# Hybrid mixer and sparse experts on one core: the output projection in three f16 products, and router logits taken from x and the mixer output

## The chip, the cores and the metric

The program runs on one core of a Trainium2 chip. The metric is the device time of one execution in microseconds; each figure is the median of several executions. The engines are TensorE (PE; PEld is its weight load), VectorE (DVE), ScalarE (ACT), GpSimd (POOL) and SyncE (SP), each with an instruction queue of its own, run in order; they meet through semaphores.

## What is computed

The reference, cut to what matters here (one sequence of 4096 tokens behind 16 learned ones, D = 1024):

```python
def hybrid_mixer(u, w_in, ..., lru_out_norm, ..., dn_out_norm, w_out):
    proj = u @ w_in                      # 3080 columns: xb gb q k v z b_logit a_logit
    y_lru = rmsnorm(rglru_group(xb, gb, ...), lru_out_norm)        # 512 wide
    y_dn = gated_deltanet_group(q, k, v, z, ..., dn_out_norm)      # 512 wide, per-head norm, times silu(z)
    return jnp.concatenate([y_lru, y_dn], axis=-1) @ w_out

h = h + hybrid_mixer(rmsnorm(h, mix_norm), ...)
h = h + hierarchical_moe(rmsnorm(h, ffn_norm), router_group_w, router_group_b,
                         router_expert_w, router_expert_b, w_gate, w_up, w_down)
out = rmsnorm(h, final_norm)[:, 16:]
```

The router takes a softmax over 4 groups, the best group, and its best two of 8 experts: 36 logits a token, from rmsnorm(h, ffn_norm) times 36 columns, plus a bias.

## The kernel before, in words

The work has four stages: a set-up, a mixer loop over 33 tiles of 128 tokens, a loop over 83 blocks of up to 128 tokens by expert, and a last loop that gathers, adds and norms the rows. The change touches the first two.

**Set-up** (L290 to L408, and the first steps of the loop). SP issues the loads of x, of w_in in six column groups, of w_out and last of the router's columns w_rt (L303). All engines then meet at a barrier (`retire`, L408). In step i = -1 the weights of w_in are split into two f16 halves in place: for each of the six groups, DVE's `scale_of` (L962) searches the largest weight, with a transpose and a one-row product on PE (`largest`, L488) to bring it across partitions; ACT's `high_halves` (L758) writes eight high halves into spare rooms; DVE's `low_halves` (L986) subtracts them; POOL copies the high halves back (L1254). Every product with w_in is then three f16 products: low weight with high x, high with high, high with low x.

**Mixer loop** (L97: steps i = -2 to 34, the middle ones in a hardware loop). One step works on five tiles at different points (class `Step`): F norms, transposes and splits x of tile i + 3; P projects tile i + 2; G runs the recurrences of tile i + 1; O multiplies the mixer output of tile i - 1 by w_out; R routes tile i - 2. All parts are active in steps 3 to 30. The order on each engine is written by hand. PE's body (L594 on) lays the six column projections (`project`, L495; L514 is its product) between the six levels of the delta rule's triangular solve: `level_y` (L569, product L580) and `level_x` (L583, product L591). In a level PE's product goes to DVE (a masked copy and a transpose, L1022 and L1028) or to ACT (a copy, L789), which return the operand of the next, while PE projects a quarter of a column group (24 products). The parts that the change touches:

- `w_out_part` (L550): 8 blocks of the mixer output times 2 halves of w_out, 16 f32 products of 512 columns (L564, two rows of the trace each) into the two banks bO. It is the last part of PE's body; the product for the norm of the recurrent branch (L752) stands behind its first eighth.
- DVE adds the bank to the residual ht (L1081), ACT norms it (L828), DVE scales it (L1110). PE transposes it in 8 products (L656, after level 2), DVE scales it by ffn_g to hT (L1146), and PE multiplies it by w_rt: 8 f32 products on 36 columns, 16 rows (L671, after level 4). DVE adds the bias (L1159) and picks groups and experts (L1165 to L1214). In the last steps, without P and G, this chain stands by itself.
- `z` is projected last, into the bank pj[1] (L531), then the 8 columns of beta and a (L546), then PE transposes x (L745). ACT's queue has, in this order: the two copies of the transposed x to f16 (L907), silu of z (L912, semaphore z_done), the square of q.
- The delta rule's output yt is transposed by PE after level 5 (L694) and copied by ACT (L876). DVE forms yl, the other half of the projection's operand, after level 3 (L1153); POOL's yg (L1290) overwrites its input and so waits for it; POOL's la (L1293) comes after yg, and ACT's square (L866), gate (L871) and tanh (L880) follow from them.

## Time and profile before

| | us |
|---|---|
| median of 3 runs | 3845.93 |
| lowest, highest | 3840.99, 3847.76 |
| profiled execution | 3841.46 |
| its span, first to last instruction | 3839.8 |
| PE busy, share of the span | 3449.2, 90% |
| DVE, ACT, POOL busy | 2168.8 (56%), 1462.9 (38%), 773.4 (20%) |
| mean granted TensorE clock | 0.961 |

The page cuts the span in 40 slices of 96 us. PE is busy 90% or more from the fourth slice to the twenty-seventh (the mixer loop) and again from the thirtieth on (the experts, where DMA is busy too); the last two slices are DMA. A timeline row merges neighbouring instructions of one line and gives the start, the length from the first start to the last end, and the count; in brackets stands the idle time before it and what ended it. Rows of PE overlap a little, so that a cost is best read from start to start.

### The profile page before, as it was taken

What the parts mean: (1) busy time and instruction counts of PE and PEld (TensorE: products, weight loads), DVE (VectorE), ACT (ScalarE), POOL (GpSimd) and SP (SyncE); (2) the same over time, 40 slices, a digit from 0 to 9 for tenths busy, and PEclk for the clock granted to TensorE, in tenths of its full rate; (3) what the DMA queues carried; (4) which work ended last, traced back from release to release, by engine and by line L of the source; (5) the groups of instructions that cost most, each with busy time, mean ns of one, the idle gap of its engine ahead of it and who ended that gap; (6) DMA issues with size and microseconds to landing.
All of it is one profiled execution on the core that took longest, in us unless ns stands there. A gap on an engine that the chain in (4) does not pass through costs nothing. (4 is left out here: it accounts for less than half of the span.)

```text
span 3839.8 us, 79823 instructions
## 1 busy us (share of the span) xinstructions
PE 3449.2 (90%) x28912; PEld 2563.9 (67%) x28913; DVE 2168.8 (56%) x6010; ACT 1462.9 (38%) x3048; POOL 773.4 (20%) x843
## 2 busy tenths in 40 slices
PE   0688999999999999999999999985899999999910
PEld 0687888888788878878887887873454454544400
DVE  4755776676677667667766776763322222222267
ACT  3444444544454444445444444532011111111168
POOL 2311221211122121212112221210111111111055
PEclk9999999999999999999999999997999999999955
DMA  5000100010010001001000100022465545456289
GB/s 197 7 7 18 49 30 33 33 44 27 33 44 33 30 30 49 27 33 44 33 27 33 49 27 33 32 90 115 153 237 204 193 153 196 153 191 224 110 337 379
DMA packets 94235, 358.72 MB, mean 93 GB/s; under 512 B 15953, under 2 KB 16210, under 8 KB 81874
## 3 DMA queue, kind: packets, MB, share of 16 engines
q1 hardware_dynamic: 49330, 219.35, 15.2%
q0 software_dynamic: 26032, 77.69, 5.7%
q10 hardware_dynamic: 18800, 60.70, 3.9%
q8 instruction: 46, 0.75, 0.1%
q14 instruction: 27, 0.22, 0.0%
HBM read 246.52 MB, written 111.18 MB: 93 GB/s over the span
## 5 line engine op out<-in xcount | busy, mean ns | idle before, releaser
L514 PE MATMUL pj<-uT,W 128*128 128x128 f16 x15840 | 979.8, 220 | 0.0
L514 PEld LDWEIGHTS pj<-uT,W 128*128 128x128 f16 x15840 | 937.4, 98 | 44.1 <-issue 38.4
L1483 PE MATMUL bA<-W,uT 128*128 x1328 | 588.6, 596 | 6.7 <-issue 4.0
L1483 PEld LDWEIGHTS bA<-W,uT 128*128 128x128 f32 x1328 | 248.2, 192 | 288.2 <-issue 288.2
L1570 DVE TENSOR_TENSOR W<-W,bA 128x256 f32<-128x256 f32 x83 | 34.9, 421 | 563.0 <-ACT W L1517 563.0
L1470 PE MATMUL pj<-W 128*128 x664 | 298.8, 593 | 1.8 <-ACT W L1522 1.8
L564 PE MATMUL bO<-W,yl 128*128 128x512 f32 x512 | 237.8, 598 | 0.0
L564 PE MATMUL bO<-W,yt 128*128 128x512 f32 x512 | 230.2, 592 | 0.0
L789 ACT ACTIVATE qh<-bA 128x256 f32<-128x256 f32 x198 | 76.6, 387 | 400.1 <-PE bA L580 400.1
L580 PE MATMUL bA<-dec,Mt 128*128 128x128 f32 x1584 | 220.4, 282 | 5.1 <-DVE dec L1028 3.3
L591 PE MATMUL bB<-X,qh 128*128 128x128 f32 x1584 | 221.0, 283 | 2.9 <-ACT qh L789 2.9
L1517 ACT ACTIVATE W<-bA 128x256 f32<-128x256 f32 x83 | 32.0, 385 | 463.5 <-PE bA L1483 463.5
L1470 PEld LDWEIGHTS pj<-W 128*128 128x128 f32 x664 | 120.1, 191 | 121.5 <-issue 121.5
L580 PEld LDWEIGHTS bA<-dec,Mt 128*128 128x128 f32 x1584 | 193.5, 193 | 8.3 <-DVE dec L1028 4.7
L591 PEld LDWEIGHTS bB<-X,qh 128*128 128x128 f32 x1584 | 193.2, 192 | 4.2 <-ACT qh L789 4.2
L1308 POOL DMA_INDIRECT idx_tab<-toki,posi x64 | 63.8, 997 | 650.5 <-DVE posi L1223 581.1
L531 PE MATMUL pj<-W,uT 128*128 128x512 f16 x792 | 191.5, 379 | 0.0
L564 PEld LDWEIGHTS bO<-W,yt 128*128 128x128 f32 x512 | 97.3, 190 | 122.4 <-issue 122.4
L1505 ACT ACTIVATE W<-pj 128x512 f32<-128x512 f32 x83 | 49.6, 597 | 329.5 <-PE pj L1470 329.5
L1022 DVE COPY_PREDICATED X<-lvl,bB 128x256 f32<-128x256 uint8 x165 | 81.6, 495 | 161.0 <-PE bB L591 159.6
L564 PEld LDWEIGHTS bO<-W,yl 128*128 128x128 f32 x512 | 93.3, 192 | 93.7 <-issue 93.7
L1545 DVE COPY W<-pj 128x512 f32<-128x512 f32 x83 | 57.4, 691 | 156.1 <-PE pj L1470 156.1
(346 smaller groups left out, 5892.1 us busy)
## 6 DMA issues: line engine op xcount, KB each, us to landing
y_rows<-W ACTq DMA_DIRECT2D x83, 512.0 KB
W<-w_gate SPq DMA_DIRECT2D x32, 1024.0 KB
W<-w_up SPq DMA_DIRECT2D x32, 1024.0 KB
W<-w_down SPq DMA_DIRECT2D x32, 1024.0 KB
x_in<-xm SPq DMA_DIRECT2D x33, 512.0 KB
ht<-xm SPq DMA_DIRECT2D x32, 512.0 KB, 3.5
h_rows<-ht SPq DMA_DIRECT2D x32, 512.0 KB, 2.6
u_rows<-ht SPq DMA_DIRECT2D x32, 512.0 KB, 2.7
```

The lines of the kernel that those rows point to most:

```text
L514: mm = pe.matmul(pj[g % 2][:, j, :], w16[:, k, w_half(w_high, COL[GROUPS[g]], 512, j * P, P)], (ul if low_u else uh)[:, k, :], start=(k == ...
L531: mm = pe.matmul(flat(pj[1]), u[:, k, :], w16[:, k, w_half(w_high, c, 512)], start=(k == 0 and n_pass == 0), stop=(k == KT - 1 and n_pass ...
L564: mm = pe.matmul(bOf[:, 512 * half:512 * half + 512], lhs, wo[:, j, 512 * half:512 * half + 512], start=(j == 0), stop=(j == 7))
L580: mm = pe.matmul(bA[:, h, :], Mt[:, h, :], T[:, h, :], start=True, stop=True)
L591: mm = pe.matmul(bB[:, h, :], Y[:, h, :], X[:, h, :], start=True, stop=True)
L789: nc.scalar.activation(first_half(Y, l), first_half(bA, l), ACT.Copy).then_inc(sem("Y_new"), 1)
L1022: a = nc.vector.copy_predicated(second_half(X, l), mask_of(l), second_half(bB, l))
L1308: pool.indirect_dma_start(out=idx_tab, out_offset=bass.IndirectOffsetOnAxis(ap=posi[:, a:a + 1], axis=0), in_=toki[:], in_offset=None).the ...
L1470: mm = pe.matmul(flat(pj[half]), hm2[:, j, :], w[:, j, 512 * half:512 * half + 512], start=(j == 0), stop=(j == 1))
L1483: mm = pe.matmul(bA[:].rearrange("p a b -> p (a b)").rearrange("p (g f) -> p g f", g=2), xT[:, k, :], w[:, k], start=(k == 0), stop=(k == ...
L1505: nc.scalar.activation(yo[par][:, 0:512], flat(pj[0]), ACT.Copy).then_inc(sem("yo_a"), 1)
L1545: nc.vector.tensor_copy(yo[par][:, 512:D], flat(pj[1])).then_inc(sem("yo_b"), 1)
```

## The change

Four things change together. w_out, times the norm gains, is split once into f16 halves in place (in step 1, half block by half block: ACT, DVE, POOL), and the mixer output is split in every tile, so that the projection is three f16 products into bO, unscaled by DVE as it adds the residual. The router's columns, times ffn_g, are folded: once through w_out (`router_through`: 8 blocks transposed by PE, copied by ACT, multiplied by PE), giving 36 more columns of the output projection, which go to pj[1]; and 36 columns on x, computed beside beta and a (44 columns in place of 8). The logits are the sum of the two, times the norm's factor. The transposes of the residual and its product with w_rt go. Beside these, buffers are renamed or shared (rnk becomes kh, hT becomes lath) and semaphores joined. The diff, cut to its core:

```diff
 # SP
                 sp.wait_ge(sem("bd_in"), 64)
+                sp.dma_start(gw, w_router.rearrange("(p k) n -> p k n", k=KT)).then_inc(sem("w_rt_in"), 16)
                 for g in GROUPS:
...
                 sp.dma_start(wo, w_out.rearrange("(k p) n -> p k n", p=P)).then_inc(sem("w_out_in"), 16)
-                sp.dma_start(w_rt[:], w_router.rearrange("(p k) n -> p k n", k=KT)).then_inc(sem("w_out_in"), 16)
...
                     if s.O:
-                        need(sp, sem("h_turned"), s.nR)
-                        settle(sp)
                         need(sp, sem("u_stored"), 32 * s.nR)
 # PE
+                def router_through(j):
+                    if j == 0:
+                        pe.wait_ge(sem("w_out_in"), 16)
+                        pe.wait_ge(sem("set_step"), GW_SET)
+                    need(pe, sem("wo_copied"), j)
+                    for k in range(KT):
+                        mm = pe.transpose((bA, bB)[k // 4][:, k % 4, :], wo[:, j, k:D:KT], ident[:])
+                    mm.then_inc(sem("wo_turned"), 1)
+                    pe.wait_ge(sem("wo_copied"), j + 1)
+                    c = 512 + (NG + NE) * j
+                    for k in range(KT):
+                        mm = pe.matmul(bOf[:, c:c + NG + NE], turned_room(j, k // 4)[:, k % 4, :], gw[:, k, :],
+                                       start=(k == 0), stop=(k == KT - 1))
+                    mm.then_inc(sem("wo_through"), 1)
...
                             need(pe, sem(free), v)
+                            if g == 1:
+                                need(pe, sem("lg_raw"), s.nR)
...
                     for k in range(KT):
-                        for n_pass, (w_high, u) in enumerate(((False, uh), (True, uh), (True, ul))):
-                            mm = pe.matmul(bB[:, 0, 0:2 * H], u[:, k, :], w16[:, k, w_half(w_high, c, 2 * H)],
+                        for n_pass, (part, u) in enumerate(((1, uh), (0, uh), (0, ul))):
+                            mm = pe.matmul(bB[:, 0, 0:2 * H + NG + NE], u[:, k, :], wba[:, k, part, :],
...
+                            need(pe, sem("h_ready"), s.nR)
+                            need(pe, sem("z_done"), s.nP)
-                        for j in (2 * m, 2 * m + 1):
-                            lhs = yl[:, j, :] if j < 4 else ydT[:, j - 4, :]
-                            mm = pe.matmul(bOf[:, 512 * half:512 * half + 512], lhs, wo[:, j, 512 * half:512 * half + 512],
-                                           start=(j == 0), stop=(j == 7))
+                        for part, whole in ((0, (False, True)), (1, (True,))):
+                            y = yl16[:, part, j, :] if j < 4 else yd16[:, part, j - 4, :]
+                            for half in range(2):
+                                for w_high in whole:
+                                    pe.matmul(bOf[:, 512 * half:512 * half + 512], y, wo16[:, j, w_half(w_high, 512 * half, 512)],
+                                              start=(j == 0 and not w_high), stop=(j == 7 and part == 1))
+                            for w_high in whole:
+                                mm = pe.matmul(pj[1][:, 0, 0:NG + NE], y, wog[:, j, 0 if w_high else 1, :],
+                                               start=(j == 0 and not w_high), stop=(j == 7 and part == 1))
...
                     if isinstance(s.i, int) and s.i == -1:
+                        largest(0, bT)
                         for g in range(len(GROUPS)):
-                            largest(g)
+                            largest(1 + g, bT)
+                            if 0 < g < 5:
+                                router_through(2 * g - 2)
+                                router_through(2 * g - 1)
+                    if isinstance(s.i, int) and s.i == 1:
+                        largest(1 + len(GROUPS), bO)
+                        largest(2 + len(GROUPS), bO)
...
                     project(s, 1, 3)
-                    if s.R:
-                        need(pe, sem("u2_ready"), s.nR)
-                        for k in range(KT):
-                            mm = pe.transpose(bO[:, k, :], ht[:, k:D:KT], ident[:])
-                        mm.then_inc(sem("h_turned"), 1)
                     level_y(s, 3)
                     project(s, 2, 0)
                     level_x(s, 3)
+                    if s.O:
+                        need(pe, sem("yt_ready"), s.nO)
+                        need(pe, sem("kd_ready"), s.nG)
+                        for h in range(H):
+                            mm = pe.transpose(bT[:, h, :], yt[:, h, :], ident[:])
+                        mm.then_inc(sem("yd_full"), 1)
...
                     level_x(s, 4)
-                    if s.R:
...
-                        for k in range(KT):
-                            mm = pe.matmul(bTf[:, 0:NG + NE], hT[:, k, :], w_rt[:, k, :], start=(k == 0), stop=(k == KT - 1))
 # ACT
+                def turned(j):
+                    act.wait_ge(sem("wo_turned"), j + 1)
+                    need(act, sem("wo_through"), j - 1)
+                    for n, bank in enumerate((bA, bB)):
+                        a = nc.scalar.activation(turned_room(j, n), bank[:], ACT.Copy)
+                    a.then_inc(sem("wo_copied"), 1)
+                def o_high(n):
...
+                    need(act, sem("o_split"), n - 3)
+                    nc.scalar.activation(o_room(n), wo[:, k, 512 * half:512 * half + 512], ACT.Copy,
+                                         scale=gso[:, k:k + 1]).then_inc(sem("o_high"), 1)
...
                             high_halves(g)
+                            if 0 < g < 5:
+                                turned(2 * g - 2)
+                                turned(2 * g - 1)
...
                     level_y(s, 3)
+                    if s.O:
+                        need(act, sem("yd_full"), s.nO)
+                        nc.scalar.activation(yd16[:, 0], bT[:], ACT.Copy).then_inc(sem("yd_high"), 1)
                     level_y(s, 4)
+                    if s.O:
+                        need(act, sem("yl_raw"), s.nO)
+                        nc.scalar.activation(yl16[:, 0], yg[:], ACT.Copy).then_inc(sem("yl_high"), 1)
...
-                        nc.scalar.activation(ydT[:], bT[:], ACT.Copy).then_inc(sem("ydT_ready"), 1)
...
+                    if isinstance(s.i, int) and s.i == 1:
+                        for n in range(16):
+                            o_high(n)
 # DVE
+                def out_scale():
+                    dve.wait_ge(sem("wo_through"), KT)
+                    step(nc.vector.tensor_reduce(wmx[:], wo, AX, ALU.max, apply_absolute_value=True))
...
+                    halves_of(wog[:], gw)
...
+                        router_columns()
                         scale_of(0)
...
+                        y_gains()
...
-                            a = nc.vector.tensor_tensor(ht[:, c], ht[:, c], bOf[:, c], ALU.add)
+                            a = nc.vector.scalar_tensor_tensor(out=ht[:, c], in0=bOf[:, c], scalar=odsc[:, 0:1], in1=ht[:, c],
+                                                               op0=ALU.mult, op1=ALU.add)
                         a.then_inc(sem("h_ready"), 1)
+                        need(dve, sem("lg_ready"), s.pR)
+                        nc.vector.scalar_tensor_tensor(out=lg[:], in0=pj[1][:, 0, 0:NG + NE], scalar=gdsc[:, 0:1], in1=lgx[:, 0, :],
+                                                       op0=ALU.mult, op1=ALU.add).then_inc(sem("lg_raw"), 1)
...
                     level_x(s, 3)
-                            a = nc.vector.tensor_tensor(hT[:, k:k + 4, :], bO[:, k:k + 4, :], rows(fg[:, k:k + 4]), ALU.mult)
                     conv(s, 1, qs, 0, 1)
-                            a = nc.vector.scalar_tensor_tensor(out=yl[:, j, :], in0=yg[:, j, :], scalar=lcol[:, 4, j:j + 1],
-                                                               in1=lrs[:], op0=ALU.mult, op1=ALU.mult)
+                        nc.vector.tensor_tensor(yg[:], yg[:], cols(lrs[:]), ALU.mult).then_inc(sem("yl_raw"), 1)
                     level_x(s, 4)
+                        nc.vector.tensor_tensor(yd16[:, 1], bT[:], yd16[:, 0], ALU.subtract).then_inc(sem("yd_ready"), 1)
                     conv(s, 1, qs, 2, 3)
+                        nc.vector.tensor_tensor(yl16[:, 1], yg[:], yl16[:, 0], ALU.subtract).then_inc(sem("yl_ready"), 1)
                     level_x(s, 5)
...
+                    if isinstance(s.i, int) and s.i == 0:
+                        out_scale()
+                    if isinstance(s.i, int) and s.i == 1:
+                        for n in range(16):
+                            dve.wait_ge(sem("o_high"), n + 1)
...
+                                                           in1=o_room(n), op0=ALU.mult, op1=ALU.subtract).then_inc(sem("o_low"), 1)
 # POOL
+                    if isinstance(s.i, int) and s.i == 1:
+                        for n in range(16):
+                            pool.wait_ge(sem("o_low"), n + 1)
+                            nc.gpsimd.tensor_copy(wo16[:, k, w_half(True, 512 * half, 512)], o_room(n)).then_inc(sem("o_split"), 1)
```

`router_columns`, `y_gains` and `out_scale` are chains of small DVE instructions, each waited for, on [128 x 8] or [128 x 288] operands, with one or two `largest` trips to PE; `out_scale` also reads all of w_out (8192 elements a partition).

## Rows read from the trace of the kernel before

**Rows 1.** Windows of the mixer stage: busy us (x instructions) by engine, granted clock.
```profile
core 0: us, PE busy (x) PEld busy (x) DVE busy (x) ACT busy (x) POOL busy (x), PEclk, DMA share, GB/s
1000.00:2000.00 1000.00, 1000.00 (x10639) 842.95 (x10637) 705.84 (x2169) 464.99 (x1021) 197.31 (x187) 1.00 0.09 35
```

**Rows 2.** Timeline of PE over one tile: start us, length us, line, tiles, xcount.
```profile
1000.95 1.11 PE L656 MATMUL bO<-ident,ht 128*128 128x128 f32 x8
1001.90 1.06 PE L580 MATMUL bA<-dec,Mt 128*128 128x128 f32 x8
...
1011.00 1.87 PE L671 MATMUL bT<-w_rt,hT 128*128 128x36 f32 x16
1012.70 1.14 PE L677 MATMUL bC<-xc,wr_bd 128*128 128x128 f32 x8
...
1038.77 1.46 PE L531 MATMUL pj<-W,uT 128*128 128x512 f16 x6
1040.07 0.75 PE L546 MATMUL bB<-W,uT 128*128 128x8 f16 x24
1040.67 0.69 PE L745 MATMUL bC<-ident,x_in 128*128 128x128 f32 x4
...
1041.63 1.88 PE L564 MATMUL bO<-W,yl 128*128 128x512 f32 x4
...
1048.73 3.60 PE L564 MATMUL bO<-W,yl 128*128 128x512 f32 x8
1052.16 3.60 PE L564 MATMUL bO<-W,yt 128*128 128x512 f32 x8
```

**Rows 3.** Timeline of PE in an early tile that has no residual yet.
```profile
188.06 1.50 PE L514 MATMUL pj<-uT,W 128*128 128x128 f16 x24
189.89 1.16 PE L580 MATMUL bA<-dec,Mt 128*128 128x128 f32 x8 [0.33 <-DVE dec L1028]
```

**Rows 4.** Timeline of ACT behind the transposes of x, tile of rows 2.
```profile
1041.83 0.60 ACT L907 ACTIVATE uT<-bC 128x512 f16<-128x512 f32 x1 [6.12 <-PE bT L745]
...
1042.80 0.69 ACT L912 ACTIVATE zs<-pj,dsc 128x512 f32<-128x512 f32 x1
```

**Rows 5.** Timelines of DVE and of PE at level 2 of the tile above.
```profile
1070.50 0.68 DVE L1122 TENSOR_TENSOR ot<-bA,eg 128x512 f32<-128x512 f32 x1
...
1071.33 1.13 PE L580 MATMUL bA<-dec,Mt 128*128 128x128 f32 x8
```

**Rows 6.** Timeline of DVE in the set-up and at the start of step 1.
```profile
51.75 4.41 DVE L973 TENSOR_REDUCE wmx<-W 128x8 f32<-128x4096 f32 x1
...
58.14 0.16 DVE L980 TENSOR_SCALAR dsc<-bT 128x1 f32<-128x1 f32 x1 [0.67 <-PE bT L493]
...
240.36 0.16 DVE L1042 SCALAR_TENSOR_TENSOR g<-al,ga 128x4 f32<-128x4 f32 x1 [6.08 <-ACT ga L805]
```

**Rows 7.** Timelines of ACT in the set-up and of PE in the last steps.
```profile
63.29 0.71 ACT L764 ACTIVATE vt<-W,gs 128x512 f16<-128x512 f32 x1
...
2622.23 1.97 PE L656 MATMUL bO<-ident,ht 128*128 128x128 f32 x8 [6.11 <-DVE ht L1110]
2625.58 3.63 PE L671 MATMUL bT<-w_rt,hT 128*128 128x36 f32 x16 [1.38 <-DVE hT L1146]
```

**Rows 8.** Timeline of SP: the last DMA that it issues before the loop.
```profile
36.47 3.67 SPq L303 DMA_DIRECT2D w_rt<-w_router  x1
```

**Rows 9.** Timeline of PE behind two idle times, and a window (columns: rows 1).
```profile
137.79 2.08 PE L677 MATMUL bC<-xc,wr_bd 128*128 128x128 f32 x8 [3.95 <-DVE xc L951]
...
162.36 1.12 PE L605 MATMUL bA<-rnq,ones 128*128 128x512 f32 x2 [1.41 <-ACT rnq L915]
...
135.00:146.00 11.00, 8.21 (x80) 8.14 (x81) 10.72 (x36) 1.80 (x7) 2.85 (x4) 0.69 0.01 2
```

**Rows 10.** Timeline of POOL beside DVE's eight subtractions, and behind them.
```profile
122.15 5.85 POOL L1254 COPY W<-rnq 128x512 f16<-128x512 f16 x1 [8.12 <-DVE W L991]
127.95 0.61 POOL L1254 COPY W<-rnk 128x512 f16<-128x512 f16 x1
```

More of the change, by code:

```diff
@@ L189, in hymba_block @@
         fg = sb("fg", [P, KT])
-        dng = sb("dng", [P, P])
+        dnc = sb("dnc", [P, 1])
+        gain = sb("gain", [P, KT])
+        gso = sb("gso", [P, KT])
+        sd = sb("sd", [P, 1])
+        rdsc = sb("rdsc", [P, 2])
+        odsc = sb("odsc", [P, 2])
+        gdsc = sb("gdsc", [P, 2])
         nexp_a = sb("nexp_a", [P, H])
@@ L916, in body @@
                         need(act, sem("conv"), 16 * s.nP)
[L917 removed]
+                        nc.scalar.activation(vs[:], vs[:], ACT.Silu).then_inc(sem("qkv_silu"), 1)
                     nc.scalar.preload_act_table_set("natural_log_exp_and_others")
```

283 lines of the change are left out of this document (170 added, 113 removed).

## The prediction, made before the result was known

> **What bounds the kernel now.** I read the windows by stage first, then the timeline of TensorE (PE) over one token tile, then ACT and DVE beside it. Between 1000 and 2000 us PE is busy 1000 of 1000 us at a granted clock of 1.00, DVE 706 and ACT 465 [rows 1]. So in the mixer stage, which covers some 33 token tiles and about 2600 us, every microsecond that leaves PE's stream leaves the time, as long as nothing new makes PE wait. The expert stage and the last stage run the same code after the change and are costed at nothing. The edit touches three places: the tile loop (32 times), the set-up before it, and the last two steps.
>
> **The tile loop, what is removed.** The output projection is 16 f32 products of 512 columns, each shown as two rows. Eight rows start 3.43 us apart [rows 2], so 32 rows are 13.7 us a tile. It becomes 48 f16 products of 512 columns. Six such products (z's, L531) take 1040.07 - 1038.77 = 1.30 us, 0.216 each, weight loads included [rows 2]: 48 are 10.4 us. The 24 router products on 36 columns are bounded by the 24 on 8 columns (1040.67 - 1040.07 = 0.60 us, 25 ns each) and by the 128-column f16 product: 24 of them fill a row of 1.50 [rows 3], and a row's length counts some 0.16 that the next start overlaps (L531's is 1.46 long, 1.30 to the next start), so 56 ns each. That is 0.6 to 1.3 us. I take 0.6, because 36 columns are nearer to 8 than to 128. Projection: 13.7 - 11.0 = **2.7 us saved**. The eight transposes of the residual (L656) go: 0.95 us (1000.95 to 1001.90). The router's 16 rows (L671) go: 1.70 us (1011.00 to 1012.70) [rows 2]. The beta columns grow from 8 to 44: 0 to 0.7 us by the same two bounds, I take 0. The mixer's transposes only move from after level 5 to after level 3. Gross: **5.4 us a tile**.
>
> **The tile loop, what it adds.** (1) The new logits go to pj[1], the bank that holds z. So the output projection now waits for z_done, and z_done is the activation that ACT issues after its two copies of the turned x. PE starts the projection at 1041.63 [rows 2], right behind the transposes of x; ACT starts the copies at 1041.83 and ends z at 1042.80 + 0.69 = 1043.49 [rows 4]. ACT's order cannot change, as its queue has the copies first. PE therefore stands still about **1.9 us** in each tile that projects, with everything behind it. What follows is a projection shorter by 2.7 us, so the next tile's start comes only 0.8 us earlier and ACT's chain (v's silu, the norms) still ends in time. (2) The transposes at L656 stood between one quarter of a projection and level 3. Three early tiles have no residual yet and show the gap without them: PE starts 24 products at 188.06 and the level only at 189.89, idle 0.33 for DVE's transpose [rows 3]; with the overlap of 0.16 that is lost too, **0.5 us** of the 0.95 comes back as a wait. (3) DVE runs without a pause into level 2: its product with eg ends at 1071.18 and PE's level starts at 1071.33 [rows 5]. The new DVE instruction that scales the logits stands ahead of it, and a small one that reads PSUM takes 0.16 [rows 6]: **0.2 us**. (4) The rest I cost at nothing. DVE loses two 512-column passes and four short ones, and gains two for the low halves and one for the norm; ACT swaps one copy for two. Both work under PE's products. The price if that cover goes is in the rivals. POOL's product yg, with la behind it on its queue, now waits for the low half at about level 5 instead of level 4; ACT's square, gate and tanh wait for it, and level 6 behind them. Laying the old durations end to end, ACT comes to level 6 just before PE needs it, by some tenths. SP loses one wait and issues the same DMAs.
>
> Per full step 5.4 - 1.9 - 0.5 - 0.2 = **2.8 us saved**. Full steps (all parts active) are i = 3 to 30: 28 x 2.8 = 79 us.
>
> **The edges of the loop.** Step 2: 2.7 - 1.9 = 0.8. Step 31, without x to turn, has almost no z wait: about 4. Steps 32 and 33 save the projection only: 5.5. In the last two steps PE waits, and the chain residual, transposes, hT, router lies open: the transposes start at 2622.23 and the router rows end at 2625.58 + 3.63 [rows 7]. That is 7 us gone from the last step, and 5 from the one before, which gets the new low halves in exchange. Sum 22 us saved.
>
> **The set-up, what it adds.** (a) DVE folds the router first: a dozen small instructions of 0.16 to 0.2, two trips to PE of 0.5 to 0.7 [rows 6], and passes over 288 columns of at most 0.5 each: +4.5 us in a stretch where DVE is the only bound. (b) w_rt was the last DMA that SP issued, and its issue took 3.67 [rows 8], while all engines wait for SP: now it is the first, so -3 (bounds 0 and -3.7). (c) Between the searches for the largest weight, PE turns two blocks of w_out and multiplies them, with ACT's copies between, four times. Such a gap is some 12.5 us of DVE work (a reduction of 4.41, eight subtractions of 0.7, a dozen small ones). ACT is free about 7 us into it, after its eight halves (the last at 63.29 [rows 7]). Then follow a copy pair (1.1), 16 router rows at the low clock (3.63), eight transposes (1.9) [rows 7], copies, 16 rows: 11 us, or 9 if the clock rises in between. So DVE waits about 4.5 us each time (bounds 0 and 6): +18. (d) Four more small instructions and some waits: +1. (e) At the end of step 0 DVE searches w_out: as much as two reductions of 4.41 [rows 6], some 18 small ones and four trips to PE, 16 us in all. DVE was idle 6.08 us there [rows 6], which leaves 10; and the next step's first two products, 512 columns each and some 1.1 us long [rows 9], now stand behind it at the low clock: +13 (bounds 8 and 16). (f) At the end of step 1, 16 half blocks go from ACT to DVE to POOL through four rooms. But POOL's copy of a half block, 0.61 alone, took 5.85 us while DVE ran eight such subtractions, 0.73 each [rows 10]. If the engines overlapped, DVE would set the pace, 16 x 0.73 = 12 us; one after the other they take 21. The row says the second, and ACT's 0.6 hides beside them: less the two or three us in which the next step's start waits for ACT's table load anyway, +16 (bounds 11 and 20). Rule of the Trainium skill, page "SBUF — State Buffer", section "Who interferes with whom": DVE with two SBUF inputs and GpSimd lock each other out for a whole instruction. By that rule this term is at its upper half, not at 11, and the row agrees with it.
> Set-up: 4.5 - 3 + 18 + 1 + 13 + 16 = **+49.5 us**.
>
> **Sum:** 49.5 - 79 - 22 = -52 us, rounded. The profiled execution took 3841.46 (span 3839.8), so it would take 3789; it stands 4.5 under the median of the three runs shown, 3845.93, and against that median I forecast **3793**.
>
> **The rivals.**
> *The clock falls at the new wait (slower).* After PE had idled 1.41 us its next two rows of 512 columns took 1.12 in all, about what they take at a granted clock of 1.00 (0.43 from start to start, and the end of the last); after 3.95 us, eight products took 2.08 instead of 1.14 [rows 2, 9], and the mean granted clock of that stretch of 11 us was 0.69, a mix of 1.2 and 2.4 GHz: up to 3.4 us of work lost. The new wait of 1.9 lies between the two idle times, nearer the harmless one. If it does cost 3 us each, 29 waits are +87: 3880. From 1.8 us a wait it eats the whole gain. Behind it: the Trainium skill, "TensorE: Matmul & The Clock Gate", Part 1, says that the clock is throttled unless activity holds it open; no row shows it doing so at 1.9 us. Chance 0.10.
> *More cover gone.* If the late yg, or DVE before levels 5 and 6, lacks its slack, PE waits another 1 us a tile, and the set-up terms come out near their upper ends: +28 and +14, 3835. For it: DVE is already the last to arrive at level 2 [rows 5]. Against: no level from 4 to 7 lets PE wait now [rows 1]. Chance 0.16.
> *The z wait costs nothing*, because what follows waits anyway: 28 x 1.9 = 53 less, 3740. Against it: PE never waits between 1000 and 2000 us [rows 1]. Chance 0.06.
> *The products are not cheaper*: if f16 weight loads showed between products, 0.1 us each, 48 would cost 15 us, not 10.4, and nothing is gained on PE: about 3920. L531's products, which load weights each time too, speak against it [rows 2]. Chance 0.02.
>
> **How the numbers follow.** The forecast has 0.66. Its own unknowns (set-up 20 to 64, gain a step 1.6 to 3.3) rarely all fall on one side: 3768 to 3820. Stretching to the cases beside it, with some 0.1 left out above and 0.08 below, gives 3760 to 3838. A measurement of this kernel can tell about 0.2%, 7.7 us. Faster: 0.66 + 0.06 + 0.12 of the third case = 0.84; same 0.05; slower 0.11.
>
> **What would show it.** PE's rows: 48 f16 rows of L564's kind at 0.216; a wait of 1.9 on ACT's z once a tile, the largest new wait; 0.5 on DVE at level 3; steps about 72.1 us apart. Before 400 us: DVE waits of 4 to 5 us on PE four times, and the first output projection about 50 us later than before. The granted clock stays near 1.00 between 400 and 2500 us. Wrong it would be if steps are over 74 us apart, if the clock falls, or if the set-up costs over 64 us.

## The result, and the profile after

The kernel after takes 3881.44 us (median of 4 runs, 3880.08 to 3885.57), the kernel before 3846.28 in the same comparison: a ratio of 1.0096, 95% interval 1.0078 to 1.0113. The change makes it slower by about 35 us, or 1%, where 53 us less were forecast.

Lines of its page, and of the page of before the one for the instruction queue, which nothing ahead of the prediction looked at:

```profile
span 3879.5 us, 81931 instructions
PE 3350.6 (86%) x29625; PEld 2503.3 (65%) x29626; DVE 2220.5 (57%) x6133; ACT 1512.9 (39%) x3145; POOL 805.3 (21%) x859
PEclk9988999999999999999999999997899999999955
q8 instruction: 282, 4.62, 0.5%
```

```profile
q8 instruction: 46, 0.75, 0.1%
```

PE is busy 99 us less than before (3350.6 against 3449.2): the work that was to go did go. But the span grew by 39.7. So the question is not what the new products cost but what PE now waits for. The window of [rows 1] gives the size of it:

```profile
1000.00:2000.00 1000.00, 937.61 (x10730) 792.23 (x10728) 707.50 (x2196) 476.16 (x1039) 199.53 (x184) 1.00 0.11 37
```

PE was never idle there before; now it is idle 62.4 us in 13.3 steps, 4.7 a step. The granted clock is 1.00 as before (the upper level, 2.4 GHz), so nearly all of the loss is idle time and not a slower clock. The waits of PE say where it is (what waited and its line, what ended the wait, us in total, times, longest). In them ot is DVE's product with eg, ahead of level 2, and dec is its transpose inside a level:

```profile
PE bO L604 <- ACT zs L976: 53.7, 30, 1.8
PE bA L623 <- DVE ot L1259: 41.8, 30, 1.8
...
PE bB L652 <- issue: 28.2, 26, 1.4
...
PE bA L623 <- DVE dec L1152: 16.1, 36, 1.7
```

Four waits, each once a step. The first was forecast at 1.9 us and is 1.84; the last at 0.33 and is 0.35. The second was forecast at 0.2 and is 1.38. The third wasn't forecast. Timeline of PE around the output projection, in a step of the loop; it answers to [rows 2]:

```profile
1015.51 0.76 PE L583 MATMUL bB<-wba,uT 128*128 128x44 f16 x24
...
1016.64 0.61 PE L781 MATMUL bT<-ident,x_in 128*128 128x128 f32 x4
1019.10 1.02 PE L604 MATMUL bO<-W,yl 128*128 128x512 f16 x4 [1.84 <-ACT zs L976]
1019.96 0.21 PE L607 MATMUL pj<-wog,yl 128*128 128x36 f16 x2
...
1030.34 0.18 PE L607 MATMUL pj<-wog,yt 128*128 128x36 f16 x1
1031.61 1.10 PE L652 MATMUL bB<-kh,ones 128*128 128x512 f32 x2 [1.09 <-issue]
```

```profile
1055.59 1.02 PE L602 MATMUL bB<-rnk,ones 128*128 128x512 f32 x2
```

The last row is of before. Read them from start to start. From the second four transposes of x to the first product of the next step are 1031.61 - 1016.64 = 14.97 us; before, the same stretch took 1055.59 - 1041.20 = 14.4. It should have been shorter by 2.6 (f16 in place of f32) and longer by 1.9 (z). It is some 1.3 us longer again, of which 1.09 is idle time ahead of L652, which is the first instruction of the hardware loop's body, and "issue" means that no semaphore of another engine explains it.

And DVE with POOL ahead of level 2, which answers to [rows 5] (L1244 is u2, the scaling of the residual; L1246 multiplies the logits by the norm's factor and adds the bias):

```profile
1045.21 0.73 DVE L1244 TENSOR_SCALAR ht<-ht,hst 128x1024 f32<-128x1024 f32 x1
1045.86 1.27 DVE L1246 SCALAR_TENSOR_TENSOR lg<-lg,hst,rb 128x36 f32<-128x36 f32 x1
...
1048.08 0.68 DVE L1259 TENSOR_TENSOR ot<-bA,eg 128x512 f32<-128x512 f32 x1
```

```profile
1045.32 1.75 POOL L1424 TENSOR_TENSOR gx<-gx,hh 128x512 f32<-128x512 f32 x1 [4.42 <-ACT hh L898]
```

The new operation on 36 columns takes 1.27 us, longer than u2 on 1024. It ends at 1047.13, where POOL's product ends (1045.32 + 1.75 = 1047.07).

The stores of h on SP's queue date the steps (the MOVE is in the loop's 27 steps alone):

```profile
L483 SPq DMA_DIRECT2D h_rows<-ht x32: 333/356/365, 442.7 to 2698.7; - x32
L483 SPq MOVE h_rows<-ht x27: 29/29/29, 516.5 to 2469.2; - x27
```

A step of the loop lasts (2469.2 - 516.5) / 26 = 75.10 us, against (2414.5 - 465.3) / 26 = 74.97 before. One by one, 24 of these steps last 74.7 to 75.3, 75.0 in the middle, and two last 76.4 and 76.7. The first store comes at 442.7 in place of 390.3. So the sum is: set-up +52.4, the 31 steps between first and last store -5.5, what follows the last store -7.2, together +39.7. Of the -5.5, the 26 steps of the loop give +3.5 and the five stretches beside them -9.0.

### The profile page after: what moved, and what is told of

It reads as the page before. It is cut to its first block and busy times, and to the rows that moved or that the text cites. A ratio compares the mean times of both kernels' runs of the same rounds, so it can differ in the third digit from the quotient of the medians.

```text
span 3879.5 us, 81931 instructions
## 1 busy us (share of the span) xinstructions
PE 3350.6 (86%) x29625; PEld 2503.3 (65%) x29626; DVE 2220.5 (57%) x6133; ACT 1512.9 (39%) x3145; POOL 805.3 (21%) x859
## 3 DMA queue, kind: packets, MB, share of 16 engines
q8 instruction: 282, 4.62, 0.5%
## 5 line engine op out<-in xcount | busy, mean ns | idle before, releaser
L604 PE MATMUL bO<-W,yl 128*128 128x512 f16 x768 | 189.6, 386 | 53.7 <-ACT zs L976 53.7
L604 PE MATMUL bO<-W,yt 128*128 128x512 f16 x768 | 179.7, 377 | 0.0
L1440 POOL TENSOR_TENSOR yg<-hh,gg 128x512 f32<-128x512 f32 x33 | 42.0, 1273 | 643.1 <-DVE yl L1287 626.0
L604 PEld LDWEIGHTS bO<-W,yl 128*128 128x128 f16 x768 | 59.7, 98 | 99.0 <-issue 61.7
```

The source lines that it names most:

```text
L604: pe.matmul(bOf[:, 512 * half:512 * half + 512], y, wo16[:, j, w_half(w_high, 512 * half, 512)], start=(j == 0 and not w_high), stop=(j == ...
```

## The experiments

All are compared with the kernel before on the same chip (3840 to 3843 us). A time "against after" sets a median beside 3881.44. The kernel before took 3846 beside that run, so such a difference is uncertain by some 5 us: by their distances from before, e1 gains 12 us and not 16, e3 gains 29 and not 34, and e4 loses 24 and not 19.

**Is it the fetching of instructions, at the loop's edge?** The after kernel's PE loop has more instructions: the profile counts 795 products and 793 weight loads in a step before, 812 and 810 after; with its waits and register instructions the body is 1625 instructions before and 1659 after (counted, as its place is, in the compiled program, which no view of the profile shows). The instruction queue moves 236 packets more, 4.62 - 0.75 = 3.87 MB, or 16.4 KB a packet. Between 1000 and 2000 us it is 118 packets, 8.9 a step, where the kernel before has none. So I moved the loop without changing it. Why its place is counted in blocks of 256 instructions is said with the third position.

```diff
+                    if isinstance(s.i, int) and s.i == -1:
+                        for _ in range(320):
+                            pe.wait_ge(sem("x_in"), 16)
                     if s.G:
```

> The kernel after, with 320 waits on a semaphore that is long full (160 instructions of TensorE in the compiled program) ahead of the loop, in the set-up, where TensorE waits anyway. Nothing in the loop changes: its 1659 TensorE instructions only lie 160 places further on, so that they begin 14 and not 110 instructions behind a multiple of 256. Theory (the loop's instructions are fetched again in every iteration because of where they lie): the 1.09 us ahead of the product of L652 (L655 here) goes in every iteration, the instruction queue moves under 60 packets instead of 282, and the time falls by 1.24 x 26 = 32 us, to about 3850. Rival (TensorE is late there for work of its own at the loop's edge, such as its registers, or for a wait that the profile doesn't name): both stay, 3881 within 5.

3865.12 us, ratio 1.0059 (1.0046 to 1.0073): 16 less than after. The wait ahead of the loop's first product is gone and the fetches with it:

```profile
q8 instruction: 49, 0.80, 0.1%
```

The waits that move the loop cost 7.4 us in the set-up (first store of h at 450.1), which I hadn't priced. The rest that it misses shows in the steps, read from the stores of h on SP's queue:

```profile
523.96 0.36 SPq L483 DMA_DIRECT2D h_rows<-ht  x1
597.68 0.35 SPq L483 DMA_DIRECT2D h_rows<-ht  x1
673.04 0.36 SPq L483 DMA_DIRECT2D h_rows<-ht  x1
```

A step is either 73.73 long, 1.25 less than after and just what the fetch was to cost, or 75.40: 18 of the first kind and 8 of the second. The timeline of PE and the window of a long step say why it is 1.67 longer:

```profile
1022.37 1.84 PE L604 MATMUL bO<-W,yl 128*128 128x512 f16 x4 [1.84 <-ACT zs L979]
1024.01 0.26 PE L607 MATMUL pj<-wog,yl 128*128 128x36 f16 x2
```

```profile
1020.00:1030.00 10.00, 8.16 (x44) 3.96 (x43) 6.79 (x26) 4.83 (x11) 2.01 (x2) 0.83 0.19 53
```

The first four products behind z's wait take 1.64 us from start to start, and 0.86 in the step of after shown above: the clock fell to its lower level (0.83 is the mean of the two levels over that stretch) behind the 1.84 us of idle time. It does so in 8 steps of 26, and in 2 of the kernel after (76.4 and 76.7). So the theory holds, with half of the gain that it gave (16 us of 32), and a second, smaller thing came out. The other direction, with the kernel before (128 waits, 64 instructions; 32 and 16 in e10):

```diff
                         for g in range(len(GROUPS)):
                             largest(g)
+                        for _ in range(128):
+                            pe.wait_ge(sem("x_in"), 16)
```

> The kernel before, with 128 waits on a semaphore that is long full (64 instructions of TensorE in the compiled program) ahead of the loop. The loop's 1625 instructions are the same, and lie 64 places further on: they end 1 instruction behind a multiple of 256 instead of 63 ahead of one. Theory (it is the place of the loop that makes it be fetched again): an idle time of about 1 us appears ahead of the product of L602 in every iteration, the instruction queue moves some 230 packets more (46 before), and the time rises by 20 to 35 us, to about 3875. Rival (the loop before is short enough wherever it lies, or the fetches are not what TensorE waits for): 3846 within 5, and 46 packets.

3882.75 us, ratio 1.0102 (1.0088 to 1.0117): **the kernel before loses 41 us, more than the whole change does, by the place of its loop alone.** (The waits themselves cost nothing: the first store of h comes at 390.2, as before.) The queue moves 280 packets. But the idle time is not where the theory had it. There is none at the loop's edge; PE waits for ot, and DVE ahead of it for the store of h:

```profile
1002.57 0.36 SPq L461 DMA_DIRECT2D h_rows<-ht  x1
...
1007.42 0.94 DVE L1112 TENSOR_SCALAR ht<-ht,hst 128x1024 f32<-128x1024 f32 x1 [1.08 <-DMA h_rows<-ht]
...
1009.33 0.67 DVE L1124 TENSOR_TENSOR ot<-bA,eg 128x512 f32<-128x512 f32 x1
...
1010.14 1.13 PE L580 MATMUL bA<-dec,Mt 128*128 128x128 f32 x8 [1.26 <-DVE ot L1124]
```

```profile
h_rows<-ht SPq DMA_DIRECT2D x32, 512.0 KB, 4.6
```

The last column is the median from issue to landing: 4.6 us, and 2.6 in the kernel before. A packet of instructions moves between 1003 and 1004, on top of the store. u2 overwrites what is being stored, so it waits, and level 2 behind it. In 24 steps of 26 this makes 76.3 to 76.4 us of 75.0; in the two others PE waits 2.49 us there, the clock falls behind it, and they last 79.2. A third position, 16 instructions on (32 waits):

> The kernel before with its loop moved on by 16 TensorE instructions (64 in e2_before_shifted). It tells how near the kernel before lies to the edge: its loop ends 63 instructions ahead of a multiple of 256 without fetches, the kernel after 24 ahead of one with them; here it is 47. If the edge is below 47: 46 packets of the instruction queue and 3843. If above: some 280 packets and 3870 or more.

Here the two parts of the question come apart:

```profile
q8 instruction: 280, 4.59, 0.5%
```

```profile
1065.02 0.36 SPq L461 DMA_DIRECT2D h_rows<-ht  x1
```

The fetches are there as expected, but not the 3870 us or more: the time is 3838.96 (one run), no longer than before, with the store landing in 2.6. No packet of instructions moves between 1064 and 1068, where this store does. So fetching again can cost nothing; where it costs, it does so at the loop's edge (after, e4) or beside a store (e2). The place that decides: in all these kernels the body touches seven blocks of 256, or eight in e2. Without fetches it ends 63, 120 and 132 instructions ahead of the next multiple (before, e1, e5), with fetches 47 and 24 ahead of it and 1 behind (e10, after, e2). The edge for seven blocks lies between 47 and 63. The Trainium skill, "Runtime: NRT & Kernel Launch", section "Instruction fetch mechanics", has PE's instruction memory as 2048 instructions, refilled sequentially in 16 KiB blocks of 256 instructions, with a fetch when a taken branch goes to a page outside the current window of two. The runs agree with the block (a packet is 16.4 KB) and with a delay at the branch (1.09 us ahead of the loop's first product). They differ on the window: the loop before touches seven blocks and is not fetched again at all. And they add that a body of 1625 instructions, well under 2048, is already at the edge. That the eighth block is kept for reading ahead is my reading of it and isn't shown; nor is what the packets beyond the seven blocks hold, as 8.9 move in each step.

**Is it the second operation on the logits, and why does it take 1.27 us?**

```diff
-                        need(dve, sem("lg_raw"), s.nR)
-                        nc.vector.scalar_tensor_tensor(out=lg[:], in0=lg[:], scalar=hst[:, 1:2], in1=rb[:], ...
...
                     if s.R:
 
+                        need(dve, sem("lg_raw"), s.nR)
+                        nc.vector.scalar_tensor_tensor(out=lg[:], in0=lg[:], scalar=hst[:, 1:2], in1=rb[:], ...
                         need(dve, sem("lg_ready"), s.nR)
                         link(s, nc.vector.tensor_copy(rg8[:, 0:NG], lg[:, 0:NG]), 1)
```

> The kernel after, with VectorE's second operation on the logits (lg times the norm plus the bias) moved from behind u2 to just ahead of the router's chain, some 20 us later, where GpSimd runs less. Theory (it is this operation's 1.27 us beside GpSimd's product that makes level 2 late): the operation takes 0.2 to 0.3 us at its new place, the wait of L623 on ot falls from 1.38 to about 0.3, and the time falls by about 1.1 x 28 = 31 us, to 3850. Rival (ot waits for GpSimd or for the products, and the operation only fills the wait): ot still ends at the same place, under 5 us gained.

3847.88 us, ratio 1.0017 (1.0008 to 1.0026): 34 less than after, forecast 31. The wait for ot is 0.20 in the step read, and 20 of 26 steps last 73.5 to 74.2, some 1.3 less than after; the others, where the clock falls as in e1, 75.2 to 75.5. At its new place the operation takes 0.69, not the 0.2 to 0.3 expected: a product of POOL's (L1443, 1059.11 to 1060.15) runs there too, and the operation, begun at 1059.51, ends with it at 1060.20. But nobody waits for it. Then the cause of the length:

```diff
-                        nc.vector.scalar_tensor_tensor(out=lg[:], in0=lg[:], scalar=hst[:, 1:2], in1=rb[:], ...
+                        nc.vector.tensor_scalar(lg[:], lg[:], hst[:, 1:2], None, ALU.mult).then_inc(sem("lg_ready"), 1)
```

> The kernel after, with VectorE's second operation on the logits at its own place behind u2, beside GpSimd's product of gx and hh, but as a product with a column alone, so that it reads one SBUF tile (36 columns) instead of two. It leaves out the router's bias. Theory (an operation of VectorE with two inputs in SBUF waits until GpSimd's, which has two as well, is over: 1.27 us for 36 columns): with one input it takes 0.1 to 0.3 us, the wait of L623 on ot falls from 1.38 to about 0.3, and the time is that of e3_logits_later, about 3848. Rival (the operation is long because of its place behind u2, for instance since it waits for u2's last writes): it still takes over 1 us, and the time stays 3881.

3880.22 us, ratio 1.0098 (1.0082 to 1.0113): a miss. By tile (min/median/max in ns):

```profile
L1246 DVE TENSOR_SCALAR lg<-lg,hst x32: 235/1252/1258, 447.8 to 2702.5; 128x36 f32<-128x36 f32 x32
```

One input does not help. Two theories were left: that this form, too, takes turns with POOL, or that the place behind u2 is the cause. Swapping the two tells them apart.

```diff
+                        need(dve, sem("lg_raw"), s.nR)
+                        nc.vector.scalar_tensor_tensor(out=lg[:], in0=lg[:], scalar=hst[:, 1:2], in1=rb[:], ...
                         need(dve, sem("h_stored"), 16 * s.nR)
                         nc.vector.tensor_scalar(ht[:], ht[:], hst[:, 1:2], None, ALU.mult).then_inc(sem("u2_ready"), 1)
-                        need(dve, sem("lg_raw"), s.nR)
-                        nc.vector.scalar_tensor_tensor(out=lg[:], in0=lg[:], scalar=hst[:, 1:2], in1=rb[:], ...
```

> The kernel after, with VectorE's second operation on the logits ahead of u2 instead of behind it: both stay beside GpSimd's product of gx and hh, which starts 0.11 us after u2 did. Theory (VectorE and GpSimd take turns here, and the one that comes second waits until the other is over): the operation starts before GpSimd's and takes 0.25, u2 then comes behind GpSimd's product and waits for its end in place of it (1.5 us or more instead of 0.73), ot comes as late as before, and the time stays 3881 within 8. Rival (the operation is long since it stands behind u2 and reads what is late there): 0.25 for it, 0.73 for u2, and 3850 as with e3_logits_later.

3881.62 us, ratio 1.0107 (1.0090 to 1.0124), and both operations as the theory said:

```profile
L1244 DVE SCALAR_TENSOR_TENSOR lg<-lg,hst,rb x32: 232/235/793, 446.6 to 2693.6; 128x36 f32<-128x36 f32 x32
L1247 DVE TENSOR_SCALAR ht<-ht,hst x32: 740/1780/1787, 446.7 to 2694.6; 128x1024 f32<-128x1024 f32 x32
```

The 1 us sticks to whichever of the two begins while POOL's product runs. The trace of after has the other proof: in the last step no POOL product is near, and the same instruction behind the same u2 takes 0.25.

```profile
2701.39 0.75 DVE L1244 TENSOR_SCALAR ht<-ht,hst 128x1024 f32<-128x1024 f32 x1 [2.64 <-DMA h_rows<-ht]
2702.05 0.25 DVE L1246 SCALAR_TENSOR_TENSOR lg<-lg,hst,rb 128x36 f32<-128x36 f32 x1
```

The Trainium skill, "SBUF — State Buffer", section "Who interferes with whom", says that a DVE instruction with two SBUF inputs contends with a GpSimd instruction that reads SBUF, that the lock is exclusive and held for the whole instruction, that issue order decides who blocks, and that a tensor_scalar can need it too, in its two-port modes. These runs agree: 1.27 us (two inputs), 1.25 and 1.78 (tensor_scalar) beside the product, 0.25 without it for the first. e8's forecast left the last point out.

**Can z's wait be taken away?** The 24 small products go behind all 48 large ones.

```diff
                             need(pe, sem("h_ready"), s.nR)
-                            need(pe, sem("z_done"), s.nP)
...
-                            for w_high in whole:
-                                mm = pe.matmul(pj[1][:, 0, 0:NG + NE], y, wog[:, j, 0 if w_high else 1, :],
...
+                    if parts[-1] == 7:
+                        need(pe, sem("z_done"), s.nP)
+                        for j in range(8):
+                            for part, whole in ((0, (False, True)), (1, (True,))):
+                                y = yl16[:, part, j, :] if j < 4 else yd16[:, part, j - 4, :]
+                                for w_high in whole:
+                                    mm = pe.matmul(pj[1][:, 0, 0:NG + NE], y, wog[:, j, 0 if w_high else 1, :],
...
```

> The kernel after, with the 24 small products of a tile (36 columns each) behind all 48 of the output projection instead of in between, and the wait for the gate z (which frees their PSUM bank) ahead of them alone. Theory: ScalarE's gate is done about 1.9 us after TensorE reaches the projection, and the 48 products take 10.4, so the wait of 1.84 at L604 goes whole and nothing takes its place: 1.9 x 30 = 55 us less, 3826. Rival (VectorE's and ScalarE's work behind the projection is late by as much, so that the time comes back as a longer wait at L623 or L652): under 20 us less.

3900.42 us, ratio 1.0150 (1.0137 to 1.0164): **slower** than after by 19, where 55 less were expected. The wait for z is gone as expected (it is not among PE's waits), but another took its place:

```profile
1022.30 0.61 PE L784 MATMUL bT<-ident,x_in 128*128 128x128 f32 x4
1022.75 1.46 PE L603 MATMUL bO<-W,yl 128*128 128x512 f16 x6
...
1033.33 0.46 PE L611 MATMUL pj<-wog,yl 128*128 128x36 f16 x12
1033.64 0.46 PE L611 MATMUL pj<-wog,yt 128*128 128x36 f16 x12
1037.56 1.10 PE L655 MATMUL bB<-kh,ones 128*128 128x512 f32 x2 [3.47 <-issue]
```

Ahead of the loop's edge stand 24 products of 26 ns, and the idle time there is 3.47 us, not 1.09. In e2 eight f32 rows of 0.43 us stand there, and it is 0. So it seems that the longer the last instructions take, the more of the fetch is hidden behind them; between after and e4 nothing else in the loop differs. The balance is -2.0 for z and +2.4 here, and the shortest steps are indeed those of after (74.9 to 75.4, 14 of 26). The other 12 last up to 78.4: behind the idle time at the edge (3.4 us on average, at most 3.7) the clock falls more often, at a price of up to 3.4 us in a step, and that makes most of the 19 us. If that is right, e4's order is good and only needs a loop that isn't fetched again (149 instructions, 300 waits at the very start):

```diff
                 def body(s):
+                    if isinstance(s.i, int) and s.i == -2:
+                        for _ in range(300):
+                            pe.wait_ge(sem("x_in"), 16)
                     if isinstance(s.i, int) and s.i == -1:
```

> The small products behind the projection with the wait for z there, as in e4_z_wait_later, and the loop moved on by 149 TensorE instructions as in e1_after_moved, with the waits that move it at the very start, where TensorE is idle until 41.2 us anyway. Theory (the 3.47 us ahead of the loop's first product in e4 are the fetch of the loop's start, all of it visible because TensorE's queue runs dry in the 24 short products): no fetches, so those 3.47 us go whole, and so does z's wait; a step lasts 75.10 - 0.85 (what e1 gained) - 1.84 (z) = 72.4 us, and the time is 3881 - 22 - 55 = 3804. Rival (the order of the small products costs it, whatever is fetched: they run slower in a row, or wait for their operands): most of the 3.47 stays, and the time is 3860 or more.

3831.01 us, ratio 0.9968 (0.9959 to 0.9977): 50 less than after and 12 less than before. The fetch was the cause, and with it and z's wait gone the clock doesn't fall either: all 26 steps last 72.88 to 72.93.

```profile
1011.97 1.46 PE L603 MATMUL bO<-W,yl 128*128 128x512 f16 x6
...
1022.86 0.46 PE L611 MATMUL pj<-wog,yt 128*128 128x36 f16 x12
1023.33 1.10 PE L658 MATMUL bB<-kh,ones 128*128 128x512 f32 x2
```

The stretch from the projection to the next step's first product is 11.36 us here and 14.81 in e4. The 27 us that it misses of the forecast are the 300 waits (first store of h at 450.7, 9.4 later than e4's 441.3: they held PE until 52.6 where it was idle to 41.2) and a step of 72.92, not 72.4: POOL's dec (0.25) and ACT's vt (0.36) are late at L670 and L697 now, since PE comes sooner. The two make 9.4 + 14 = 23; the last 4 stay unexplained.

**Together.** First the three repairs, e5's and e3's diffs in one kernel:

> e5_z_later_moved with VectorE's second operation on the logits moved as in e3_logits_later (which gave 34 us). The three losses are of different places of a step, so their prices should add: 3804 - 34 = 3770, a step of 71.2 us, below the kernel before by 72 us. Rival (they overlap; with one gone the chain of VectorE is the bound): 3785 or more.

3792.08 us, ratio 0.9873 (0.9857 to 0.9888): 39 less than e5. The number lies in the rival's range, but the steps go from 72.9 to 71.7 (forecast 71.2), so the logits' place adds as expected, and the sum stays above 3770 because e5 did by 27.

Then a fourth, the transposes of yt ahead of level 3's first product:

```diff
                     project(s, 1, 3)
+                    if s.O:
+                        need(pe, sem("yt_ready"), s.nO)
+                        need(pe, sem("kd_ready"), s.nG)
+                        for h in range(H):
+                            mm = pe.transpose(bT[:, h, :], yt[:, h, :], ident[:])
+                        mm.then_inc(sem("yd_full"), 1)
                     level_y(s, 3)
                     project(s, 2, 0)
                     level_x(s, 3)
-                    if s.O:
...
```

> e6_all_three with the turning of yt (4 transposes, 0.45 us of TensorE) ahead of level 3's first product instead of behind its second. Level 3's wait for VectorE's transpose (0.35 us, 36 times in the profile after) is then covered: 10 us less than e6, 3760. Rival (level 3's second product, which then has less behind it, or VectorE, late by the same, takes it): the same as e6.

3782.24 us, ratio 0.9851 (0.9836 to 0.9866). The wait for DVE's transpose at level 3 is gone from the loop (6 times left of 36), 10 us; the two intervals overlap, but the steps show it clearly: 71.29 us in place of 71.73.

Last, the waits that move the loop put where PE is idle in steps 1 and 2:

```diff
-                    if isinstance(s.i, int) and s.i == -2:
-                        for _ in range(300):
-                            pe.wait_ge(sem("x_in"), 16)
...
+                    if isinstance(s.i, int) and s.i in (1, 2):
+                        for _ in range(200 if s.i == 1 else 100):
+                            pe.wait_ge(sem("x_in"), 16)
```

> The kernel of e7_all_three_and_turn, with the 300 waits that move the loop taken from the very start (where they held TensorE until 52.6 instead of 41.2 us) and put where TensorE waits for VectorE's scale of w_out in steps 1 and 2 (15.8 and 9.3 us idle). The first store of h comes 8 to 9 us sooner (450.3 in e7), the steps stay 71.3 us: 3774. Rival (the waits are in the way there too): 3782 or more.

**3775.00 us, ratio 0.9822 (0.9808 to 0.9835)**: first store of h at 440.2, steps of (2366.2 - 512.8) / 26 = 71.28 us, all between 71.26 and 71.30. This version beats the kernel before by 67 us and the one after by 106, with the same arithmetic as the change.

```profile
PE bC L697 <- ACT vt L900: 15.1, 30, 4.8
PE bA L626 <- DVE ot L1262: 11.4, 30, 1.5
PE bC L670 <- POOL dec L1417: 8.5, 29, 0.5
```

These three, about 1 us a step, are what is left.

## Why the prediction was wrong

The forecast was 3793 (range 3760 to 3838, slower 0.11); 3881 came. Set against its own sum:

**What held.** The removed work and its price: e4 shows 48 large products, 24 small ones and the ones-product in 1022.75 to about 1033.95, so 11.0 without the last, as forecast; 44 columns instead of 8 cost nothing (0.60 from start to start). (1), the wait for z: 1.84 against 1.9. Level 3: 0.35 idle, about 0.5 with the lost overlap, as forecast. The set-up: +52.4 to the first store of h against some 48.7 (49.5, less 0.8 for step 2). Its parts are nearly right: DVE waits for PE four times behind `router_through`, 6.27 us in place of 0.47 each time, +23 (forecast +18, its upper bound 24); step 1 begins its level 3 81.9 us after step 0's (70.1 before: +11.8, forecast +13 for the search of w_out), step 2 another 86.2 (69.3 before: +16.9, forecast +16 for the split); and folding the router with the earlier DMA, (a) and (b), forecast at +1.5, costs nothing (the first of the six searches comes back to DVE at 56.99, and at 57.02 before).

**What held in part.** The stretches beside the loop's 26 steps, from the first store to the end, save 9.0 + 7.2 = 16.2 us, where 79 + 22 - 73 - 0.8 = 27 were forecast. Most of the lack is in the last two steps, for which 12 us had been priced as an open chain that goes: PE now waits 10.1 and 9.0 us there for DVE (L759, on the router's ohs), where it waited 2.6 and 4.2 before. So what left the chain came back in part as a longer wait behind it.

**The step that failed** is the net gain of a full step, "5.4 - 1.9 - 0.5 - 0.2 = **2.8 us saved**". It is nothing: 75.10 on average against 74.97, which over 26 steps is 76 of the 92 us between the forecast change of the span (-52) and the measured one (+39.7); the stretches beside them are 11 more and the set-up 4. Two terms of it:

1. *Term (3), "the new DVE instruction that scales the logits stands ahead of it, and a small one that reads PSUM takes 0.16 [rows 6]: 0.2 us".* It measured 1.4 to 1.5, and e3 got back 1.3 a step, 34 us in all. There are two new operations on the logits, and I priced the one that reads PSUM (0.24 in fact). The other reads SBUF and lands on POOL's product. I had used the lock rule for the split of w_out in the set-up, and had not asked here what POOL does in that microsecond. The trace of before had the answer: that product there started while u2 ran and took 1.59 us in place of 1.27:

```profile
1068.82 0.73 DVE L1110 TENSOR_SCALAR ht<-ht,hst 128x1024 f32<-128x1024 f32 x1
```

```profile
1069.09 1.59 POOL L1277 TENSOR_TENSOR gx<-gx,hh 128x512 f32<-128x512 f32 x1 [4.28 <-ACT hh L839]
```

2. *"(4) The rest I cost at nothing."* A longer PE body was not in my list at all. It costs 1.09 idle a step at the loop's edge, and 1.25 with the lost overlap (e1). Nothing in PE's rows of before showed it: at the places tried, the fetches are either all there or not at all, by where the loop ends in the instruction stream. What could have been seen is the instruction queue, which moves nothing between 1000 and 2000 us before, and that the body grows by 34 instructions.

Together with z and level 3 the sum is 1.84 + 1.09 + 1.38 + 0.35 = 4.66 idle a step, and some 0.16 more at each of the four starts: 5.3, of 5.25 saved (2.6 + 0.95 + 1.70). The two terms explain the miss of a step: 75.0 - 1.25 (e1) - 1.3 (e3) = 72.4, where 72.1 was forecast with z's and level 3's waits in it. The forecast's condition "steps over 74 us apart" is what came.

**The rivals.** "The clock falls at the new wait" gave 3880, and 3881 was measured: nearly right in number, and for another reason. It supposed 3 us of work lost at each of 29 waits. In the kernel after the clock falls in 2 steps of 26 and costs 1.4 to 1.7 us each. But it isn't nothing either: the same wait costs 8 x 1.67 = 13 us in e1. The forecast's reading "nearer the harmless one" was right of most steps. "More cover gone" had the place (DVE before level 2, 1 us) and 3835 for it; with e1's price of the fetch on top (1.25 x 26 = 32) that is 3867. "The products are not cheaper" is off in its own sum: 0.1 us on 48 products in 28 steps is 134 us, so 3927 and not 3920; nothing hangs on it. That two losses add, each from a cause of its own, was in none of the cases, and 0.66 was too much for a step priced from durations laid end to end.

**What stays open.** Why the clock falls in some steps of the same idle time and not in others; that it is the instruction packet which delays the store in e2 (the trace shows that they overlap, and that the delay is gone where they don't, not on which DMA engine they meet); and what the eighth block is for. Not tried: w_out in f16 products with the old router, which would have neither z's wait nor the second operation on the logits, and would lose what the new logits save a step (2.65 us of L656 and L671, less 0.6 for the small products).

## What to carry to other kernels

When a loop fills one engine, a change of its instruction count is a term of the sum: look at the instruction queue's packets inside the loop, before and after, and if they appear, move the loop by some instructions in the prologue (at a place where the engine is idle) before judging the change itself. Price an added VectorE operation by what GpSimd runs at that moment, not by its size. And where a wait is removed and the time rises, as in e4, look for the wait that took its place before giving the idea up: with the second cause gone the same edit gave 35 us (e5 against e1, each by its distance from before).

## What the runs showed of the hardware

A loop whose body is fetched again in each iteration costs between nothing (e10: 280 packets, 3838.96 us) and 3.5 us an iteration (e4), and the cost goes with how much work stands ahead of the branch (0.6 us of short products in e4, 3.4 us of f32 rows in e2, which has no idle time there) and with whether a 16 KB packet meets a store that an engine waits for (landing 4.6 us instead of 2.6, e2). Moving the loop by 64 instructions changed a kernel by 41 us with no other edit. Waits on a full semaphore are not free in bulk either: 320 of them held TensorE 17 us in e1, which is 53 ns each, and 128 of them 6.4 us in e2, 50 ns each. In e1 the profile puts the time down to POOL, but the kernel after has no wait at this place:

```profile
155.57 17.79 PE L552 MATMUL pj<-uT,W 128*128 128x128 f16 x288 [17.02 <-POOL W L1404]
```

And TensorE's clock falls now and then behind one and the same idle time: with 1.84 us of it a step in 2 steps of 26 (after), 6 (e3) or 8 (e1), 1.4 to 1.7 us lost each time; with 2.49 us in both steps of e2 that had it; with 3.4 us on average in about half of them (e4); in none of 26 where no single wait in the loop is over 1.5 us (e5, e9). A mean granted clock of 0.99 over 1000 us, which looks like nothing, was about 1 us a step in e4:

```profile
1000.00:2000.00 1000.00, 933.25 (x10667) 794.13 (x10666) 700.68 (x2161) 474.38 (x1038) 201.42 (x187) 0.99 0.10 36
```
